# Projection of prompt tiles 4 to 7 moved out of its own phase into the background of the expert gathers, in plain float32

## The reference, cut to what matters

```
m = silu(c) W_ada + b_ada                    -> shift1, scale1, gate1, shift2, scale2, gate2
h = rmsnorm(x) * (1 + scale1) + shift1
z = h W_in                                   # 7168 columns: q | k | v | gMLP u, v | gates A, B
q, k = rope(rmsnorm(q)), rope(rmsnorm(k))    # 8 heads x 2 maps x 64
A = differential attention(q, k, v)          # softmax map 1 - lambda * map 2, causal
B = u * (tril(W_s) v + b)                    # within 128-row chunks
x = x + gate1 * (sigmoid(g_A) (A W_A) + sigmoid(g_B) (B W_B)) W_o
h2 = rmsnorm(x) * (1 + scale2) + shift2
s = product-key scores of h2 W_q             # 8 heads, 2 x 128 keys, top 16 -> 128 experts per row
x = x + gate2 * sum_e g_e gelu(u_e . h2) v_e # rows u_e, v_e gathered from 16384-row tables
```

## Time and profile before

| | us |
|---|---|
| median of 3 runs | 4627.4 (4611.09 to 4628.77) |
| span of the profiled execution | 4635.2 |
| projection, first to last product | 116 to 829 |
| front of the tail (attention 0, mix 0, samples) | about 840 to 1400 |
| first selection of experts, alone | about 1400 to 1476 |
| gathers with background | 1476 to the end |

### The profile page before, as it was taken

One profiled execution on the slowest core, in us unless ns is written; L12 is line 12 of the kernel. 1 busy time (PEld: TensorE's weight loads), 2 busy tenths in 40 slices (PEclk: granted clock), 3 DMA queues, 4 the chain that ended last, 5 costly groups with the idle time before them and its releaser, 6 DMA issues.

```text
span 4635.2 us, 46840 instructions
## 1 busy us (share of the span) xinstructions
PE 2910.9 (63%) x16545; PEld 1758.9 (38%) x16545; DVE 2580.5 (56%) x5693; ACT 587.0 (13%) x1207; POOL 2652.2 (57%) x2513
## 2 busy tenths in 40 slices
PE   2999999896892766777375644554535346333355
PEld 1777777564771652434143322322301113000011
DVE  2666542342116896997675448467466556657511
ACT  0211133332010012333000100001000000000000
POOL 2232231234222567877677668667677677777776
PEclk7999999887895887888688776776767656656656
DMA  7323221789875999999999999999999999999999
GB/s 281 122 98 122 99 75 66 263 326 366 332 255 201 369 374 412 378 367 401 414 408 420 419 418 354 410 419 414 412 382 415 388 419 419 410 416 389 363 417 363
DMA packets 468722, 1550.19 MB, mean 334 GB/s; under 512 B 51638, under 2 KB 108407, under 8 KB 453084
## 3 DMA queue, kind: packets, MB, share of 16 engines
q0 software_dynamic: 351376, 1271.99, 69.7%
q1 hardware_dynamic: 116268, 262.92, 14.9%
q10 hardware_dynamic: 864, 12.58, 0.7%
HBM read 1482.18 MB, written 65.23 MB: 334 GB/s over the span
## 4 chain that ended last, share of the span: by engine, by line
POOL 32%; DMA 19%; PE 14%; issue 11%; DVE 5%; POOLq 1%; SPq 0%; ACT 0%; DVEq 0%; ACTq 0%
POOL u_rows L950 15%; POOL v_rows L964 14%; DMA v_rows<-in_peer_v,expertsT 13%; PE ps_y L1290 5%; POOL v_rows_extra L964 3%; DMA u_rows<-in_peer_u,experts 3%; PE ps_bank L1143 2%; DVE u_rows L1860 2%; DMA v_rows<-in_cache_v 2%; PE ps_bank L1149 1%; PE ps_bank L1067 1%; DMA v_rows_extra<-in_peer_v,expertsT 1%; PE ps_y L1248 1%; PE ps_bank L1070 1%; PE ps_y L1207 0%
## 5 line engine op out<-in xcount | busy, mean ns | idle before, releaser
L1860 DVE CUSTOM_DVE_ANT_0 u_rows<-u_rows,h_rows 128x1024 f32<-128x1024 f32 x1056 | 1292.5, 1225 | 1071.0 <-DMA u_rows<-in_peer_u,experts 899.4
L1290 PE MATMUL ps_y<-v_rows,w_columns 128*32 128x512 f32 x3552 | 700.7, 930 | 1145.9 <-DMA v_rows<-in_peer_v,expertsT 1107.1
L950 POOL DMA_INDIRECT u_rows<-in_peer_u,experts x1024 | 1096.7, 1071 | 457.4 <-issue 293.5
L964 POOL DMA_INDIRECT v_rows<-in_peer_v,expertsT x888 | 972.3, 1095 | 428.3 <-issue 249.8
L1290 PEld LDWEIGHTS ps_y<-v_rows,w_columns 128*32 128x32 f32 x3552 | 139.4, 145 | 1567.6 <-issue 1565.9
L302 PE MATMUL ps_z<-w_in_high,hT_high 128*128 128x512 f32 (+1 forms) x1008 | 399.7, 397 | 0.0
L302 PE MATMUL ps_z<-w_in_high,hT_low 128*128 128x512 f32 (+1 forms) x1008 | 397.8, 395 | 0.0
L302 PE MATMUL ps_z<-w_in_low,hT_high 128*128 128x512 f32 (+1 forms) x1008 | 396.2, 393 | 0.0
L279 POOL CAST w_in_high<-w_in_buf 128x4096 fp32r<-128x4096 f32 x14 | 50.4, 3602 | 454.7 <-PE ps_z L302 430.6
L1149 PE MATMUL ps_bank<-turned_a,weights 128*128 128x256 f32 (+1 forms) x1280 | 270.5, 371 | 0.9 <-ACT turned_a L1313 0.9
L1143 PE MATMUL ps_bank<-weights,turned_a 128*128 128x256 f32 (+1 forms) x1152 | 268.1, 393 | 1.8 <-ACT turned_a L1313 1.8
(11 more groups left out here) (241 smaller groups left out, 3727.9 us busy)
## 6 DMA issues: line engine op xcount, KB each, us to landing
u_rows<-in_cache_kT POOLq DMA_DIRECT2D x128, 512.0 KB, 6.1
v_rows<-in_cache_v POOLq DMA_DIRECT2D x128, 512.0 KB, 6.5
weights<-in_peer_w_q SPq DMA_DIRECT2D x40, 1024.0 KB, 7.8
w_in_buf<-in_w_in POOLq DMA_DIRECT2D x14, 2048.0 KB, 9.4
scratch_z<-z_out SPq DMA_DIRECT2D x112, 256.0 KB, 2.0
weights<-in_w_att_out SPq DMA_DIRECT2D x20, 1024.0 KB, 18.2
weights<-in_w_gm_out SPq DMA_DIRECT2D x20, 1024.0 KB, 8.1
weights<-in_w_out SPq DMA_DIRECT2D x20, 1024.0 KB, 7.9
```

The source lines that it names most:

```text
L950: pool.indirect_dma_start(ur[:, slot, :], None, g.peer_u, bass.IndirectOffsetOnAxis(ap=col, axis=0)).then_inc(s_ur[slot], 16)
L964: pool.indirect_dma_start((vx if other else vr)[:, slot, :], None, g.peer_v, bass.IndirectOffsetOnAxis(ap=idxT[:, t % 3, k:k + 1], axis=0) ...
L1290: last = nc.tensor.matmul(ps_y[32 * j:32 * (j + 1), b:b + CB], wcol[:, base:base + 32], (vx if four[j][0] else vr)[:, four[j][1], b:b + CB ...
L1860: nc.vector.tensor_tensor_reduce(ur[:, slot, :], ur[:, slot, :], hrow[:, t % 2, :], 1.0, 0.0, ALU.mult, ALU.add, a[:, s:s + 1]).then_inc(s ...
```

## The change: what it does

The projection phase computes only tiles 0 to 3 and 8 (`FIRST`), with a ring of 5 banks in place of 6; `w_in` is laid out in 28 chunks of 256 columns so that both phases can read it, and the matmul reads its 512 columns from two chunks. Tiles 4 and 5, then 6 and 7 (`LATER`) are projected by a new kind of background step, `proj`, 37 steps per group: square, norm and transposes of two tiles, then 28 units, each one chunk of 1 MB by both tiles in plain float32 matmuls (no high and low parts), with the evacuation, norm, rotation and stores of z. It has 3 weight slots. Attention goes in four pairs of tiles instead of two groups of four; only the first is in `FRONT`. Several semaphores are merged, with the same waits in other counts.

```diff
+BLOCKS = (4, 0, 5, 1, 6, 2, 7, 3, 10, 8, 11, 9, 12, 13)
+FIRST = (0, 1, 2, 3, 8)
+LATER = ((4, 5), (6, 7))
 def projection_phase(nc, g):
-    RING = 6
-    STEPS = 2 * TILES
+    RING = 5
+    N1 = len(FIRST)
+    STEPS = 2 * N1
...
-                    pool.dma_start(w_raw[:], w_view[:, :, b * CB:(b + 1) * CB]).then_inc(s_wl, 16)
+                    pool.dma_start(w_raw[:], w_view[:, 2 * b:2 * b + 2]).then_inc(s_wl, 16)
...
-                            last = nc.tensor.matmul(ps_z[0:r, (b * TILES + t) % RING, :], hT[lhs][:, k, t * P:t * P + r],
-                                                    w[rhs][:, b, k, :], start=k == 0 and (lhs, rhs) == (0, 0),
+                            last = nc.tensor.matmul(ps_z[0:r, (b * N1 + t) % RING, :].rearrange("p (h c) -> p h c", h=2),
+                                                    hT[lhs][:, k, t * P:t * P + r], w[rhs][:, b, :, k, :], start=k == 0 and (lhs, rhs) == (0, 0),
                                                     stop=k == KD - 1 and lhs == 1)
...
-GROUPS_ATT = ((0, 1, 2, 3), (4, 5, 6, 7))
+GROUPS_ATT = ((0, 1), (2, 3), (4, 5), (6, 7))
...
-    BACK = ((every("mix", 1), 0, 35),
-            (every("att", 1) + every("mix", 2), 35, 116),
-            (every("mix", 3), 116, 168),
-            (every("mix", 4), 168, 220))
-    LATE = (3,)
+    BACK = ((every("att", 1) + every("mix", 1), 0, 40),
+            (every("proj", 0), 40, 66),
+            (every("att", 2) + every("mix", 2), 66, 114),
+            (every("proj", 1), 114, 138),
+            (every("att", 3) + every("mix", 3), 138, 179),
+            (every("mix", 4), 179, 222))
+    LATE = (3, 5)
...
+                def pw_load(p, c):
+                    slot = (p * CHUNKS + c) % WP
+                    if c >= WP:
+                        filled(sp, ("P", p, (c - WP + 1) * len(LATER[p]) // 2 - 1))
+                    sp.dma_start(pw[:, slot], g.w_in[c]).then_inc(s_pw[slot], 16)
...
+                def z_store(p, u):
...
+                    src = pzo[:, j, :].rearrange("p (t c) -> p t c", t=2)
+                    sp.dma_start(g.z[t * P:(t + 2) * P, col:col + QB].rearrange("(t p) c -> p t c", p=P), src).then_inc(s_pst[j], 16)
+                    if blk in (2, 3, 4, 5):
+                        keep = g.o_kp if blk < 4 else g.o_vp
+                        sp.dma_start(keep[t * P:(t + 2) * P, col % D:col % D + QB].rearrange("(t p) c -> p t c", p=P), src).then_inc(s_pst[j], 16)
...
+                def proj(p, k):                      # SP
+                    L, K0, U = len(LATER[p]), proj_lead(p), proj_units(p)
+                    if k == 0:
+                        done = LATER[p][0]
+                        sp.wait_ge(s_xst, 16 * 2 * done)
+                        for b in range(2):
+                            sp.wait_ge(s_sst[b], 16 * 4 * done)
+                        for i in range(2):
+                            px_load(p, i)
+                        for n in (1, 0):
+                            sp.dma_start(pmod[:, n, :], g.mod[0:1, n * D:(n + 1) * D].broadcast_to([P, D])).then_inc(s_pc, 16)
+                        for c in range(WP):
+                            pw_load(p, c)
...
+                        if tl[0] not in FIRST:       # att, k == 0
+                            for j in range(PR):
+                                sp.wait_ge(s_pst[j], stored_after[group_of(tl[0])][j])
...
+                def proj(p, k):                      # PE, the units
...
+                        for i in range(2):
+                            cols = slice((2 * pair + i) * P, (2 * pair + i + 1) * P)
+                            for kk in range(KD):
+                                last = nc.tensor.matmul(dst[:, i * QB:(i + 1) * QB], phT[:, kk, cols], pw[:, slot, kk, :],
+                                                        start=kk == 0, stop=kk == KD - 1)
+                        fills(last, ("P", p, u))
...
+                def rotate(p, u, quarter):           # DVE, of 8 q and k units per group
...
+                    if quarter == 0:
+                        dve.wait_ge(s_psd, raw)
+                        link(nc.vector.reciprocal(prs[:, 0:m], psd[:, 0:m]))
+                        link(nc.vector.tensor_tensor(z3, z3, prs[:, 0:m].unsqueeze(2).broadcast_to([P, m, wd]), ALU.mult))
...
+                    if quarter == 1:                 # gain, cosine
...
+                    if quarter == 2:                 # two half-wide sine products
...
+                        nc.vector.tensor_tensor(pzo[:, j, :], pt1, pt2, ALU.add).then_inc(s_pzo, 1)
```

More of the change, by code:

```diff
@@ L227, in projection_phase @@
                 acts += 1
[L228 to L231, removed]
+            units.append((kind, block, n % N1, n % RING, raws, acts, before))
+        w_view = g.w_in.rearrange("a p k c -> p a k c")
+        x_dram = [g.x_prompt[t * P:(t + 1) * P, :] if t < PT else g.x_sample for t in FIRST]
+        rows_at = lambda i: rows_of(FIRST[i])
+        NCONST = 16 * (N1 + 3)
         with nc.Block() as block:
@@ L315, in _ @@
                 pe.wait_ge(s_inp, 48)
-                for t in range(TILES):
+                for t in range(N1):
                     turn_h(t)
@@ L329, in _ @@
                         pe.wait_ge(s_w, i * 2 + (b + 1))
-                        for t in range(TILES):
-                            product(i * STEPS + (b * TILES + t + 1), b, t)
+                        for t in range(N1):
+                            product(i * STEPS + (b * N1 + t + 1), b, t)
             @block.scalar
@@ L376, in _ @@
                 square(1)
[L377 removed]
+                for t in range(1, N1):
                     high_hT(t - 1)
[L379 removed]
+                    if t + 1 < N1:
                         square(t + 1)
@@ L382, in _ @@
                         evacuate(t - 2)
-                high_hT(TILES - 1)
-                for n in range(TILES - 2, len(units)):
+                high_hT(N1 - 1)
+                for n in range(N1 - 2, len(units)):
                     evacuate(n)
@@ L569, in units @@
                 out += [("S", p, k - 25)]
+        if kind == "proj":
+            if 0 <= k - 3 < len(LATER[p]):
+                out += [("pt", p, k - 3, f) for f in range(2)]
+            if 0 <= k - proj_lead(p) < proj_units(p):
+                out += [("P", p, k - proj_lead(p))]
         if kind == "satt":
@@ L589, in tail_phase @@
                 main += 1
+    PR, WP = 4, 3
+    LINKS = {"rope": 8, "gate_v": 3}
+    later, raws, acts, linked, stored_z, wp_loaded, wp_n = {}, 0, 0, 0, [0] * PR, {}, [0] * WP
+    for p in range(len(LATER)):
+        for u in range(proj_units(p)):
+            chunk, pair = divmod(u, len(LATER[p]) // 2)
+            blk = BLOCKS[chunk // 2]
+            kind, n = KINDS[blk // 2], len(later)
+            before, dve = stored_z[n % PR], kind in LINKS
+            stored_z[n % PR] += 32 if blk in (2, 3, 4, 5) else 16
+            raws, acts = raws + dve, acts + (not dve)
+            later[p, u] = (kind, blk, blk * CB + chunk % 2 * QB, pair, n % PR, raws, acts, before)
+        for chunk in range(CHUNKS):
+            wp_n[(p * CHUNKS + chunk) % WP] += 16
+            wp_loaded[p, chunk] = wp_n[(p * CHUNKS + chunk) % WP]
+    stored_after = {}
+    for p in range(len(LATER)):
+        after = [0] * PR
+        for q in range(p + 1):
+            for u in range(proj_units(q)):
+                after[later[q, u][4]] += 32 if later[q, u][1] in (2, 3, 4, 5) else 16
+        stored_after[p] = after
+    PL = max(len(tl) for tl in LATER)
+    zs_free, slot_raw = {}, [0] * PR
+    for key in later:
+        kind, j, raw = later[key][0], later[key][4], later[key][5]
+        if kind in LINKS:
+            zs_free[key] = slot_raw[j]
+            slot_raw[j] = raw
+    norms = [sum(len(LATER[q]) for q in range(p)) for p in range(len(LATER) + 1)]
     maxima, n = {}, 0
@@ L865, in mix @@
                             sp.dma_start(g.sc[t * P:t * P + r, b * QB:(b + 1) * QB], so[0:r, b % 2, i, :]).then_inc(s_sst[b % 2], 16)
-                background = {"att": att, "mix": mix}
+                background = {"att": att, "mix": mix, "proj": proj}
                 for kind, p, k in FRONT:
@@ L1257, in satt @@
                         fills(last, ("so", y))
-                background = {"att": att, "mix": mix, "satt": satt}
+                background = {"att": att, "mix": mix, "satt": satt, "proj": proj}
                 for kind, p, k in FRONT:
```

360 lines of the change are left out of this document (257 added, 103 removed).

## The result

The changed kernel takes 4562.75 us (median of 4 runs, 4556.42 to 4580.05) against 4628.09 before: ratio 0.9872, 95% interval 0.9840 to 0.9905.

A forecast was written before the change was run, and what follows sets the result against it. TensorE bounds the projection, DMA the gathers at 419 GB/s. Projection -312, front -48, bytes +264 and tight places +65 sum to -31 us: 4596 from a median of 4627.4, range 4515 to 4680 (the forecast's own case 4560 to 4630).

The forecast's parts named there:

- Projection, -312: Projection phase: 56 TensorE-bound units at 5.53 us leave it, so it ends at about 517 instead of 829, gaining 312 us.
- Front, -48: Front before the gathers: attention of tiles 2 and 3 leaves it, gaining 48 us, with bounds of 20 and 90.
- Bytes, +264: Gathers: repeated weights, x and tables, z with new k and v, and paired attention loads cost 264 us of DMA time.
- the term for rows of 512 bytes (59): Gathers: 12.6 MB more from attention in pairs, in 512-byte rows at 4.7 us per MB, cost 59 us.
- Tight places, +65: Four places in the gathers where added engine work does not fit: 65 us together, bounds 20 and 140.
- stage 0: First gather stage: attention of tiles 2 and 3 brings DVE to 268 us, over the stage's 257, costing 15 us.
- stage 4 with attention 3 and mix 3: Attention 3 and mix 3 pressed into 41 ticks, PE 13.6 us per tick against 13.3 of DMA: 15 us lost.
- the late stages (+20): Two late selection stages in place of one, the first also carrying rotations on DVE: 20 us lost.
- the load of the scores (+15): Scores loaded directly after the mix that makes them, three times instead of once, stopping DVE, then POOL: 15 us lost.
- A: Rival, chance 0.26: background cheaper, with small rows at full rate, tight places 25, front 60; total -122, so 4505 us.
- B: Rival, chance 0.22: TensorE at clock 0.83 bounds the compressed mix steps, 108 us in place of 25, so 4679 us.
- F: Rival set with the experiments, no chance given: the gain is the front's; attention in pairs alone gains 10 to 40 us.

The follow-up runs named there:

- pairs_only: Kernel before the change with only the attention put in four pairs of tiles, one in the front, and the matching ticks: 4666.66 us, ratio 1.0093.
- few_weights: Changed kernel with all but the first three weight chunks of each background projection loaded only to one eighth, 45.9 MB less: 4476.73 us, ratio 0.9678.
- light_proj: Changed kernel with half the background projection's matmuls and its q, k and v norms and rotations left out, same DMAs: 4546.04 us, ratio 0.9828.
- att4_front: Changed kernel with attention of tiles 0 to 3 back in the front and pairs only for the later tiles: 4557.11 us, ratio 0.9846.
- two_groups_att: Changed kernel with tiles 4 to 7 projected as one group, one late stage, and attention in two groups of four: 4501.41 us, ratio 0.9738.
- z_twice: Changed kernel with every background store of z made twice, 14.7 MB more in 1 KB rows: 4586.03 us, ratio 0.9913.

## Why the prediction was right, and which term was mis-sized

- **Projection, -312.** Last product at 517, forecast 517; 433 matmuls in 100 us make blocks of 120 matmuls 27.7 us long at full PE; POOL's cast waited for PE. Right in size and mechanism.
- **Front, -48.** First gather 359.4 us sooner where 360 was forecast, and 54 us from the front in pairs_only. Right.
- **Bytes, +264.** SP's queue shows +259 us, but for 99.9 MB: the forecast listed 95 MB and missed 5 MB. Operands of mix 1 (6.3 MB), which SP used to load ahead of the first gather, now fall behind it, and the first 1.3 MB of attention 1 are loaded ahead. Without them (12 us at the full rate) the listed bytes cost 247: the term for rows of 512 bytes (59) came out at 44. For 1 KB rows 2.9 us per MB were taken and 3.1 found on the queue. The whole execution moves 69.7 MB more (1550.19 and 1619.88 MB on the pages) where 72 to 76 were forecast, an estimate that leaves out the 2.1 MB of x that the shorter projection no longer loads. The gathers are 280 us longer, less than the 300 to 360 forecast, and less than the 264 + 65 of the sum.
- **Tight places, +65.** This is the term that was mis-sized: all that is not DMA time came to about 21 us. By the gap between the share and its full 1.03: stage 0 went from 257 x 0.08 = 21 to 289 x 0.12 = 35 us, +14 (forecast +15); stage 4 with attention 3 and mix 3 from 4 to 22, +18 (forecast +15), and the stretch 2920 to 3020, with PE at 97%, DVE at 93% and 335 GB/s, is where. Over all nine stages the same count goes from 86 to 112 us, +26. But the late stages (+20) went the other way: stage 3 from 405 x 0.03 = 12 to 450 x 0.01 = 5, stage 5 stayed at 8; and the load of the scores (+15) made DVE wait nowhere. In stage 3 it is the added traffic that hid the delay: few_weights, with nearly the same engine work and 45.9 MB less, is back at 13 us. For the other places this is argued and not shown: the stages became 10 to 17% longer, so DVE has more time per slot, and the loads of SP can keep the DMA engines busy while a gather ring stands. I had sized these places as if the bytes and the engine work added up in the same tick, and here they overlap. The sum for the late stages also took 1.3 us for a dot where the earlier trace rows have 1.22; that moves its tick of 16 us by 0.3 and changes nothing.
- **A** had the tight places right (25, and 21 to 26 found), but not the small rows (3.1 and 3.5 us per MB, not 2.4) nor the front (48, not 60). **B**: the v gathers waited 195 us more for PE, but B needs the DMA share to fall in the mix steps, and in stages 1 to 3, with a part of mix 1 and all of mix 2, it is 1.02. Only in stage 4, where mix 3 lies with attention 3, is PE nearly full for 100 us, at a clock of 0.91; that stage lost 18 us more than before, not 42. light_proj does not bear on B, since it leaves the mix steps alone. **F**, that the front gives the gain, is refuted by att4_front.
- The total: -359.4 + 279.9 = -79.5 between the profiles, 59 to 71 us faster by the runs, against -31. The difference between the profiles is 44 us of tight places and 5 of bytes. The time lies between a third and half of the way from the forecast (4596) to A (4505), at the lower end of the forecast's own 4560 to 4630; it is the wide range, which goes half way into A, that holds it.

Where the gain of 312 us went: the projection's bytes take about 200 of it back (an estimate from the prices above), the engine work 15, and the attention in pairs 42 more than its shorter front saves. That leaves some 55, beside 59 to 71 measured; the parts come from separate runs and need not add exactly.

## What to carry to other kernels

When one stage is bound by TensorE and a later one by DMA, work moved between them is worth its engine time less the bytes it brings along, at the rate of the saturated stage; count each operand once per group that reads it, and make the groups as few as the buffers allow (one group in place of two: 50 us of 4561). Work whose bytes are paid for in both places is not worth moving (att4_front). Delays of engines in a stage that is itself being lengthened by bytes can overlap with them and need not be added (stage 3 here), until the steps come so dense that the DMA share falls (two_groups_att).

## What the runs showed of the hardware

Time of SP's queue per MB, beside gathers that keep the DMA engines full: 2.4 us in 2356 to 2716, in mostly rows of 4 KB and more (67 us for 27.5 MB); 3.1 in rows of 1 KB (z_twice, 46 us for 14.7 MB); 3.2 in 1836 to 2196, where most rows have 512 bytes (31 us for 9.66 MB), and 3.5 for such rows alone, by subtraction, in pairs_only. The Trainium skill (DMA: Bandwidth & Descriptors, Specifications) gives 512 bytes as the smallest transfer at line rate. On this queue the trace does not agree: at 1 KB the price is still a quarter above that of the longest rows. But the 1 KB rows were stores and the long ones mostly loads, and no run here tells length from direction.

The rate stayed at 412 GB/s and the DMA share at 1.02 over the 472 us of stage 1 and the 450 us of stage 3, with PE busy 75% and 73% of them; a burst of background lost DMA time without any engine being full (two_groups_att: 330 GB/s at PE 84% and DVE 76%).
